# Stationary operands stored with two halves in turn: the up-projection and the second half of the down-projection read them with a step of two words

## The reference

```
gate, up = split(h @ w_up)                 # h 256 x 2048, w_up 2048 x 11264
act      = gelu(dwconv(gate)) * up         # 256 x 5632
x        = x + g2 * (act @ w_down)         # w_down 5632 x 2048
return rmsnorm(x, final_norm_g)
```

## Time and profile before

| | us |
|---|---|
| median of 2 runs | 2171.94 (2171.58 to 2172.3) |
| the profiled execution's span | 2171.5 |
| TensorE matmul busy | 2132.8 |
| TensorE weight load busy | 1987.9 |
| VectorE busy | 1464.8 |
| ScalarE busy | 1037.6 |
| start of L, of M0, of M1, end of M1's matmuls (about) | 1425, 1920, 2041, 2162 |

### The profile page before, as it was taken

The page is one execution under the profiler, slowest core; times in us unless marked ns, Lnnn a source line. Parts: engine busy times, 40 slices in busy tenths (PEclk is TensorE's granted clock), DMA queues, the critical chain, the costliest instruction groups (busy, mean ns, idle before and its releaser), DMA issues.

```text
span 2171.5 us, 38030 instructions
## 1 busy us (share of the span) xinstructions
PE 2132.8 (98%) x16496; PEld 1987.9 (92%) x16496; DVE 1464.8 (67%) x1850; ACT 1037.6 (48%) x1418; POOL 25.0 (1%) x47
## 2 busy tenths in 40 slices
PE   7999999999999999999999999999999999999998
PEld 7989999988999999998788999999999999988886
DVE  7666556666757698696665577789666665555665
ACT  6554334444454465454433455465444444444454
POOL 0000000110000000000000000000000000000000
PEclk9999999999999999999999999999999999999999
DMA  9765655775448878786565655766777775555553
GB/s 326 239 208 195 196 194 176 232 243 162 153 156 263 295 256 267 252 285 223 182 224 166 233 175 192 255 210 229 240 245 240 243 242 195 194 193 190 182 196 112
DMA packets 339156, 470.05 MB, mean 216 GB/s; under 512 B 14797, under 2 KB 312557, under 8 KB 326126
## 3 DMA queue, kind: packets, MB, share of 16 engines
q1 hardware_dynamic: 337838, 466.93, 64.5%
q0 software_dynamic: 1152, 0.70, 0.1%
HBM read 464.80 MB, written 2.10 MB: 215 GB/s over the span
## 4 chain that ended last, share of the span: by engine, by line
PE 91%; DVE 5%; ACT 2%; DMA 2%; issue 1%; SPq 0%; ACTq 0%; DVEq 0%
PE ps L1971 64%; PE ps L1982 11%; PE ps L1990 4%; DVE wlo L1191 2%; PE ps L2002 1%; PE ps L2060 1%; ACT whi L595 1%; DMA raw<-w_branch_dram 1%; PE ps L2321 1%; PE ps L2261 1%; PE ps L2223 1%; PE ps L2255 1%; DVE arena L1257 1%; DMA raw<-w_in_dram 1%; PE ps L1926 1%
## 5 line engine op out<-in xcount | busy, mean ns | idle before, releaser
L1191 DVE TENSOR_TENSOR wlo<-raw,whi 128x1024 fp32r<-128x1024 f32 (+1 forms) x668 | 814.6, 1221 | 661.7 <-ACT whi L595 658.5
L595 ACT ACTIVATE whi<-raw 128x1024 fp32r<-128x1024 f32 (+1 forms) x668 | 706.3, 1058 | 1065.2 <-PE ps L1971 860.5
L1971 PE MATMUL ps<-f_hi,whi 128*128 128x256 f32 x2112 | 422.0, 281 | 1.6 <-DVE f_lo L1835 1.6
L1971 PE MATMUL ps<-f_lo,whi 128*128 128x256 f32 x2112 | 413.8, 277 | 0.0
L1971 PE MATMUL ps<-f_hi,wlo 128*128 128x256 f32 x2112 | 413.5, 277 | 0.0
L1971 PEld LDWEIGHTS ps<-f_hi,whi 128*128 128x128 f32 x2112 | 320.7, 188 | 14.3 <-issue 11.8
L1971 PEld LDWEIGHTS ps<-f_hi,wlo 128*128 128x128 f32 x2112 | 319.9, 188 | 0.0
L1971 PEld LDWEIGHTS ps<-f_lo,whi 128*128 128x128 f32 x2112 | 319.9, 188 | 0.0
L1971 PE MATMUL ps<-phi,whi 128*128 128x256 f32 (+2 forms) x1440 | 300.7, 290 | 0.0
L1971 PE MATMUL ps<-plo,whi 128*128 128x256 f32 (+2 forms) x1440 | 288.4, 281 | 0.0
L1971 PE MATMUL ps<-phi,wlo 128*128 128x256 f32 (+2 forms) x1440 | 288.1, 281 | 0.0
(11 more groups left out here) (380 smaller groups left out, 2595.1 us busy)
## 6 DMA issues: line engine op xcount, KB each, us to landing
raw<-w_in_dram SPq DMA_DIRECT2D x151, 1024.0 KB, 5.9
raw<-ada_w_dram SPq DMA_DIRECT2D x96, 1024.0 KB, 5.0
raw<-ffn_w_up_dram SPq DMA_DIRECT2D x88, 1024.0 KB, 5.0
raw<-ffn_w_down_dram SPq DMA_DIRECT2D x44, 1024.0 KB, 5.2
raw<-w_out_dram SPq DMA_DIRECT2D x32, 1024.0 KB, 5.7
raw<-w_branch_dram SPq DMA_DIRECT2D x16, 1024.0 KB, 6.1
arena<-xT_dram SPq DMA_DIRECT2D x4, 544.0 KB, 6.6
arena<-ctxT_dram SPq DMA_DIRECT2D x1, 2048.0 KB, 11.1
```

The lines of the kernel that those rows point to most:

```text
L595: nc.scalar.activation(whi[slot_of(c)][:, 0:w], src, ACT.Copy).then_inc(S("split_hi"), 1)
L1191: v.tensor_tensor(wlo[slot_of(c)][:, 0:w], src, whi[slot_of(c)][:, 0:w].bitcast(F32), ALU.subtract).then_inc(S("split_lo"), 1)
L1971: l = mm(ps[2 * p + h][0:m, b:b + tt.stop - tt.start], wx[:, k], x[:, xi, tt], start=first, stop=last)
```

## The change

The two halves of a row of stationary weights, which the matmuls load one after the other, are stored column by column in turn: column c of half h stands at position 2c + h, where it stood at 128h + c. A load then takes every second word of 256, where it took 128 words in a row.

- In L, the high plane is stored so ("woven") in the chunks with q of 1 to 3 and the low plane in those with q of 2 and 3. ScalarE writes the high plane with a step of two words; VectorE reads the high plane and writes the low plane with it. `raw` is read as before.
- In M1 (units with i of 11 and more in `down_hi` and `down_lo`), `dhi` and `dlo` are stored so, for the two halves of the tokens.
- The matmuls' slices of the stationary operand have a step of 2 there, in `down_last` too. M0 stays as it is.

The number of instructions, of DMAs and of waits is the same.

```diff
+        def woven(v, n):
+            return v.rearrange("p (k c h) -> p k h c", k=n, h=2)
+        def halves(v, n):
+            return v.rearrange("p (k h c) -> p k h c", k=n, h=2)
+        def weave(c, low):
+            u, q = CHUNK[c]
+            return UNITS[u][0] == "L" and q >= (2 if low else 1)
...
             # hi(c), ScalarE
-                nc.scalar.activation(whi[slot_of(c)][:, 0:w], src, ACT.Copy).then_inc(S("split_hi"), 1)
+                dst = whi[slot_of(c)][:, 0:w]
+                if weave(c, False):
+                    dst, src = woven(dst, 4), halves(src, 4)
+                nc.scalar.activation(dst, src, ACT.Copy).then_inc(S("split_hi"), 1)
...
             # down_hi(u), ScalarE
+                dst, src = dhi[:, k:k + 4, :], rx(actT[:, 1024 * (i % 11):1024 * (i % 11) + 1024], 4)
+                if i >= 11:
+                    dst, src = dst.rearrange("p k (c h) -> p k h c", h=2), src.rearrange("p k (h c) -> p k h c", h=2)
+                nc.scalar.activation(dst, src, ACT.Copy)\
...
             # lo(c), VectorE
+                high, low = whi[slot_of(c)][:, 0:w].bitcast(F32), wlo[slot_of(c)][:, 0:w]
+                if UNITS[u][0] == "L":
+                    src = halves(src, 4)
+                    high = woven(high, 4) if weave(c, False) else halves(high, 4)
+                    low = woven(low, 4) if weave(c, True) else halves(low, 4)
+                v.tensor_tensor(low, src, high, ALU.subtract).then_inc(S("split_lo"), 1)
...
             # down_lo(u), VectorE
+                if i >= 11:
+                    low, high = (w.rearrange("p k (c h) -> p k h c", h=2) for w in (low, high))
+                    src = src.rearrange("p k (h c) -> p k h c", h=2)
+                v.tensor_tensor(low, src, high, ALU.subtract).then_inc(S("dn_lo"), 1)
...
             # down_last, TensorE
-                        l = mm(ps[2 * t + nb][:, :], x[:, kd, 128 * t:128 * t + 128], wx[:, 512 * nb:512 * nb + 512], start=False, stop=last)
+                        l = mm(ps[2 * t + nb][:, :], x[:, kd, t:256:2], wx[:, 512 * nb:512 * nb + 512], start=False, stop=last)
...
             # chunk(c), TensorE, L
                                 k = slice(n * k4 + 128 * h, n * k4 + 128 * h + m)
+                                if weave(c, wx is wl):
+                                    k = slice(n * k4 + h, n * k4 + UC, 2)
...
             # chunk(c), TensorE, M0 and M1
+                                rows = slice(t, 256, 2) if name == "M1" else slice(128 * t, 128 * t + 128)
+                                l = mm(ps[(4 if name == "M0" else 0) + 2 * t + nb][:, :], x[:, kd, rows],
```

More of the change, by code:

```diff
@@ L606, in down_hi @@
                 k = 4 * (u % 2)
-                nc.scalar.activation(dhi[:, k:k + 4, :], rx(actT[:, 1024 * (i % 11):1024 * (i % 11) + 1024], 4), ACT.Copy)\
+                dst, src = dhi[:, k:k + 4, :], rx(actT[:, 1024 * (i % 11):1024 * (i % 11) + 1024], 4)
+                if i >= 11:
+                    dst, src = dst.rearrange("p k (c h) -> p k h c", h=2), src.rearrange("p k (h c) -> p k h c", h=2)
+                nc.scalar.activation(dst, src, ACT.Copy)\
                     .then_inc(S("dn_hi"), 1)
@@ L1190, in lo @@
                 dve.wait_ge(S("split_hi"), c + 1)
-                v.tensor_tensor(wlo[slot_of(c)][:, 0:w], src, whi[slot_of(c)][:, 0:w].bitcast(F32), ALU.subtract).then_inc(S("split_lo"), 1)
+                high, low = whi[slot_of(c)][:, 0:w].bitcast(F32), wlo[slot_of(c)][:, 0:w]
[4 more added lines that the diff above has]
+                v.tensor_tensor(low, src, high, ALU.subtract).then_inc(S("split_lo"), 1)
             def down_lo(u):
@@ L1197, in down_lo @@
                 dve.wait_ge(S("dn_hi"), i + 1)
-                v.tensor_tensor(dlo[:, k:k + 4, :], rx(actT[:, 1024 * (i % 11):1024 * (i % 11) + 1024], 4),
-                                dhi[:, k:k + 4, :].bitcast(F32), ALU.subtract).then_inc(S("dn_lo"), 1)
+                low, src, high = dlo[:, k:k + 4, :], rx(actT[:, 1024 * (i % 11):1024 * (i % 11) + 1024], 4), dhi[:, k:k + 4, :].bitcast(F32)
+                if i >= 11:
+                    low, high = (w.rearrange("p k (c h) -> p k h c", h=2) for w in (low, high))
+                    src = src.rearrange("p k (h c) -> p k h c", h=2)
+                v.tensor_tensor(low, src, high, ALU.subtract).then_inc(S("dn_lo"), 1)
             def raw_planes(g):
@@ L1981, in chunk @@
                             for nb in range(2):
-                                l = mm(ps[(4 if name == "M0" else 0) + 2 * t + nb][:, :], x[:, kd, 128 * t:128 * t + 128],
+                                rows = slice(t, 256, 2) if name == "M1" else slice(128 * t, 128 * t + 128)
+                                l = mm(ps[(4 if name == "M0" else 0) + 2 * t + nb][:, :], x[:, kd, rows],
                                        wx[:, 512 * nb:512 * nb + 512], start=first, stop=last)
```

## The result

The changed kernel takes 2193.68 us (2191.94 to 2195.42, 2 runs) against 2171.94 us; the ratio is 1.0101 with a 95% interval of 1.0079 to 1.0123. It is slower by 1.0%, where I had forecast 0.7% faster. The time is in my range and in the class "within 2%", but on the wrong side.

A forecast was written before the change was run, and what follows sets the result against it. TensorE's matmul pace was taken to bound the kernel. From the profiled 2171.5 us, -12.5 us in L and -2.3 us in M1, with ScalarE and VectorE at 0, gave 2156.7, forecast as 2157 us; likeliest range 2148 to 2167, wider 2148 to 2202.

The forecast's parts named there:

- The bound: Whole kernel: TensorE busy for 98% of the span, so in L and the down-projection only one matmul's pace matters.
- The failed step: Woven loads of L and M1: one 4.4 ns read conflict taken off each, 12.5 and 2.3 us, together -14.8 us.
- The two levels in stretches with equal tiles: Line 1971: same tiles run at 113.3 or 117.8 ns a matmul, taken as read-stream conflicts in steps of 4.4 ns.
- The load is hidden: L: a stationary load takes at most the 113.3 ns of the 256-column matmul in which it is hidden.
- rival of the long load: L alone: stepped load outlasts its matmul; 43.4 us at 128.7 ns, 2491 us if fully doubled; chance 0.14.
- The upper bound: Stepped loads doubled to 226.7 ns: L would pay 2816 x 113.3 = 319 us and M1 nothing.
- a contiguous moving operand crosses groups at least as fast: Woven loads: memory already feeds 256 contiguous words in 113.3 ns or less, so the doubled load was not taken.
- The worse phase: Woven loads meet the moving read more often: one step up costs 12.5 + 2.3 us, 2187; two 2202; chance 0.16.
- M1: Down-projection's 528 woven loads of dhi and dlo: 4.4 ns off each, -2.3 us.
- ScalarE and VectorE at 0: Woven splits: ScalarE's writes hidden, at most +1.06 us each; VectorE's reads and writes no slower, spread about 2 ns.
- the 5.9 us of slack: L: 8.2 us for splitting a high plane, less 2.3 us of engine work, leaves 5.9 us to hide a doubled write.
- No verdict beyond 2%: Whole kernel: 0.82 for no change within about 2%, 43 us; slower 0.14, faster 0.04.

The follow-up runs named there:

- e7_half_moving: Changed kernel's stepped loads with planes stored as before the change, and L's matmuls given 128 moving columns instead of 256; 2594.41 us.

## Why the prediction was wrong

- **The bound** was read rightly: TensorE's pace alone sets L and the down-projection, and every microsecond of the change is there.
- **The failed step** is the one that took 4.4 ns off each woven load of L and M1, as a conflict that a step of two would remove, 14.8 us in all. No run shows such a removable 4.4 ns: the woven loads added 7 ns in L and 4.4 ns in M1, and a load of one single word repeated left L at 113.4 ns. What bounds L outside its first units is the pair of a load and its matmul, 111.7 ns whatever the moving columns: 224 and 128 of them left the pace where it was, and one column at 373 us in the trace of before has it too. The step adds its 7 ns to that. The two levels in stretches with equal tiles are real, and they led me to a cause for the lower one that they don't show: that a level exists above says nothing on what the floor is made of.
- **"The load is hidden"** was half of that failure. My rival of the long load wrote that it decides from 113.3 ns on and that the load is only just hidden; its mechanism was the right one, with 120 ns instead of 129 to 227. A load that is level with its matmul has no cover, so its smallest growth is paid in full: 2816 x 6.5 ns = 18.3 us where I had -12.5. That is a mean: it is 1.6 ns in the first six units, which I had priced like the others though they ran at 120 ns before.
- **The upper bound** was in its place, one step further: the doubled load (226.7 ns) came true at steps of four and eight, 233 and 241 ns. My argument that a contiguous moving operand crosses groups at least as fast held for a step of two against doubling, but it did not make the step free.
- **The worse phase** had the nearest time (2187) by the wrong cause, which was luck; a uniform weave did not bring the old pace back.
- **M1**: I had -2.3 us, measured +2.3. The load, 111.7 ns in L, is well under the 228.9 ns of 512 columns there; it is 7 ns longer by its row, and the matmul 4.4 ns slower. 96 contiguous columns gave the same 233.3 ns as the step, and a step of zero 231.7, so the number of groups is not its cause alone; it may be a level like those in the stages before. Left open.
- **ScalarE and VectorE at 0** were right: VectorE's 1225 ns did not move, as the earlier trace rows said, and ScalarE's 0.1 us an instruction was covered by its waits, as the 5.9 us of slack said.
- **No verdict beyond 2%** was right. By the estimate of the columns' time the most that could be gained is 2816 x 6.7 + 528 x 15.6 = 27.0 us, 1.2%, and the doubled load did not come at a step of two.

No run was faster than the kernel before beyond its interval, and nothing in them points to a version that would be.

## What to carry to other kernels

When weight loads and matmuls alternate with one load to each matmul, ask which of the two is longer before pricing a change to either: change the moving columns and see whether the pace follows, or look for a stretch of the trace with very few moving columns. With float32 operands and 256 columns here they were nearly level (111.7 ns, against an estimated 106.7 ns for the columns), so a load's access pattern was worth its full price, and a price of 7 ns over 2816 loads is nearly 1%. Keep the stationary operand contiguous: a step of two words cost 7 ns a load here, and steps of three, four and eight cost 60, 120 and 127 ns.

## What the runs showed of the hardware that was not expected

At half clock the load's step of two cost nothing: four chunks of L in turn (q from 0 to 3) in `e7_half_moving`, of which three have stepped loads, have the same length. From 1700 us on it is one run of 1752 matmuls in 373.76 us, 213.3 ns each, with both kinds of load.

```profile
1502.73 5.01 PE ps L1994 x24
...
1508.19 5.01 PE ps L1994 x24
...
1513.65 5.01 PE ps L1994 x24
...
1519.11 5.01 PE ps L1994 x24
```

Starts of pairs within the first are 0.43 us apart (1502.85, 1503.28, 1503.70, 1504.13 us), 213 ns each. So the 7 ns that the step of two adds at the clock 1.00 don't show at 0.50; one kernel shows it, and it was not tested further. That the kernel with half the moving columns lost TensorE's clock was not expected either: it took 2594.41 us for less work. This is what TensorE did before the clock fell:

```profile
1430.00:1433.00 3.00, 2.69 (x23) 2.54 (x22) 3.00 (x5) 1.42 (x3) 0.00 (x0) 1.00 0.84 292
1433.00:1436.00 3.00, 1.85 (x14) 1.81 (x15) 2.97 (x7) 0.84 (x1) 0.00 (x0) 1.00 0.64 190
```

It was busy for 2.69 and 1.85 of 3 us, waiting for VectorE's splits. After that both of its rows were busy for 40.00 of 40 us and more at 0.50, and the clock was back at 1.00 from about 2340 us on, with the 512 columns of M0. And loads of 64 columns were slower than loads of 128, by 5.7 ns a matmul.
